# A float32 decoder layer on one core: seven products of halves in place of eight in its projections, with the sums of the weights made on GpSimd

## The reference

```
h = rms_norm(x)
proj = h @ w_in            # (1024, 1024) x (1024, 10256)
(gq, gk, gv, g_low, gr, hq, hf, hi, hg, sz, sxbc, sdt, gates) = split(proj)
y_gla, y_hgrn, y_ssm = three mixers of these (silu of gr, hq, hg, sz; a causal convolution of 4 taps and silu on sxbc)
merged = sum of sigmoid(gates[i]) * (y_i @ w_br[i]);  x = x + merged @ w_out
h2 = rms_norm(x); router: softmax over 4 groups (top 1), 8 experts in it (top 2)
x = x + weights * SwiGLU experts of h2;   out = rms_norm(x)
```

## Time and profile before

| | |
|---|---|
| time, median of 3 runs | 2144.92 us (2144.08 to 2148.81) |
| the profiled execution | 2143.66 us, its span 2142.0 us |
| TensorE busy, weight loads busy | 1979.7 us (92%), 1621.3 us |
| VectorE, ScalarE, GpSimd busy | 1337.7, 921.4, 362.7 us |
| granted TensorE clock, mean | 0.971 |
| HBM | 211 GB/s over the span |

### The profile page before, as it was taken

One profiled execution on the slowest core, in us unless ns is written; L12 is line 12 of the kernel. 1 busy time (PEld: TensorE's weight loads), 2 busy tenths in 40 slices (PEclk: granted clock), 3 DMA queues, 4 the chain that ended last, 5 costly groups with the idle time before them and its releaser, 6 DMA issues. The chain is left out here.

```text
span 2142.0 us, 26814 instructions
## 1 busy us (share of the span) xinstructions
PE 1979.7 (92%) x10826; PEld 1621.3 (76%) x10827; DVE 1337.7 (62%) x1475; ACT 921.4 (43%) x998; POOL 362.7 (17%) x203
## 2 busy tenths in 40 slices
PE   6999999999999999999997999986699999999994
PEld 5778888888987777777775787865588888888872
DVE  5930000576215777877874565556698999999974
ACT  4211010112114444444443334231578888878863
POOL 4223232243310000000001000012122222222210
PEclk9999999999999999999998999998799999999997
DMA  5242222224236553565645754451799999999986
GB/s 160 82 157 98 99 98 79 78 79 137 80 103 151 151 165 120 147 157 161 149 121 187 258 216 162 154 206 60 293 367 382 386 391 384 388 386 388 386 328 247
DMA packets 217236, 435.97 MB, mean 204 GB/s; under 512 B 27730, under 2 KB 150754, under 8 KB 189602
## 3 DMA queue, kind: packets, MB, share of 16 engines
q1 hardware_dynamic: 185954, 361.97, 49.3%
q10 hardware_dynamic: 20288, 51.39, 6.7%
...
HBM read 369.67 MB, written 81.43 MB: 211 GB/s over the span
## 5 line engine op out<-in xcount | busy, mean ns | idle before, releaser
L636 DVE TENSOR_SCALAR tap<-u,taps 128x1024 f32<-128x1024 f32 x16 | 20.1, 1297 | 293.1 <-ACT u L594 293.1
L666 PE MATMUL ps<-h_hi,w_hi 128*128 128x512 f32 x576 | 178.1, 391 | 2.4 <-PEq L58 2.4
L666 PE MATMUL ps<-h_hi,w_lo 128*128 128x512 f32 x576 | 177.8, 390 | 0.0
L666 PE MATMUL ps<-h_lo,w_hi 128*128 128x512 f32 x576 | 177.7, 390 | 0.0
L2416 DVE TENSOR_TENSOR gu_lo<-gate_raw,gu_hi 128x2048 fp32r<-128x2048 f32 x64 | 146.6, 2293 | 32.8 <-ACT gu_hi L2361 32.7
L1311 PE MATMUL psum<-h_hi,l_hi 128*128 128x512 f32 x384 | 158.7, 413 | 3.5 <-PEq L58 3.5
L1311 PE MATMUL psum<-h_lo,l_hi 128*128 128x512 f32 x384 | 160.1, 417 | 0.0
L1311 PE MATMUL psum<-h_hi,l_lo 128*128 128x512 f32 x384 | 157.5, 410 | 0.0
L2416 DVE TENSOR_TENSOR gu_lo<-up_raw,gu_hi 128x2048 fp32r<-128x2048 f32 x64 | 146.4, 2287 | 13.7 <-ACT gu_hi L2361 13.7
L2421 DVE TENSOR_TENSOR dn_lo<-dn_raw,dn_hi 128x2048 fp32r<-128x2048 f32 x62 | 142.0, 2292 | 16.4 <-ACT dn_hi L2371 13.2
L604 ACT ACTIVATE out<-ps 128x2048 f32<-128x2048 f32 x14 | 26.4, 1883 | 270.2 <-PE ps L666 201.2
...
## 6 DMA issues: line engine op xcount, KB each, us to landing
...
```

The costliest lines, as they stand in the source:

```text
L666: ins = nc.tensor.matmul(ps[b][:, a * T + half * 512:a * T + half * 512 + 512], w[:, k, a * P:(a + 1) * P], h[:, k, half * 512:half * 512 ...
```

## The change

The weights and h are cut into halves. For one pair of 128-column tiles, the weights are four blocks of 512 rows by 128 columns, and h is four quarters of 512 channels by 512 tokens. The four output quarters came from eight products of such blocks. Now (`step` on each engine) they come from seven: of blocks and of sums and differences of blocks. The four sums of h (`th`, `tl`) are made once, by VectorE and ScalarE (`rows`, `rows_hi`, `rows_split`), those of the weights in every step by GpSimd (`summed`). Seven products (`g` 0 to 6) go to the three PSUM banks X, Y and Z; the partial sums of X and Y are read out in between, by ScalarE (snapshots) and VectorE (`added`), and the third, fifth and seventh product (`g` 2, 4, 6) wait for that (`snap_ready`, `c_ready`). ScalarE now makes the upper parts of the weights (`upper`), VectorE the rest (`lower`), and both for step n+1 while step n's products run. The silu and the convolution steps take turns (convolution at n = 1, 3, ..., 15), and the taps of step n-1 run in step n (`tap`); their first one moved to ScalarE (`conv_first`). Two of the `tokens` steps come first and two last. The four loops are written out.

Other edits: in `norm1_and_decays` two PSUM tiles take turns, and ScalarE casts two upper parts; each block makes its own `ident`; `y` and `gates` have another order in HBM, so that a load reads longer rows; in `merge_and_route` the turned rows and logits of the first chunks run one step later (`beside`), `rest_w` for the last step comes before `gated`, and records and weights of the choice are made ahead of `places`; `recs` is loaded before the work list is stored; two blocks end without the drain of GpSimd; `finish` adds chunks 2, 3, 5, 6 on TensorE and no more 1, 3, 4, 6.

```diff
+        def turn_ps(c):
+            return acc[2][:] if c < NCH // 2 and c % 2 else tr[:]
...
-            upper_part(2)
-            upper_part(3)
             upper_w(1)
             for c in range(4, NCH):
+                pool.wait_ge(hi_ready, c)
...
+            def upper_part(c):
+                act.wait_ge(hf_ready, c + 1)
+                nc.scalar.copy(h_hi[:, :, c * CH:(c + 1) * CH], h_f[c % 2][:]).then_inc(hi_ready, 1)
...
+    COLS = [TOKENS[0], TOKENS[1]] + STEPS + [TOKENS[2], TOKENS[3]]
...
+        X, Y, Z = ([ps[b][:, i * S:(i + 1) * S] for b in range(2)] for i in range(3))
...
+        def source(n, g):
+            return (block_of(n, 0, 0), sum_w, sum_w, block_of(n, 0, 1), block_of(n, 1, 0), block_of(n, 0, 1), block_of(n, 1, 1))[g]
...
+            def summed(n, i):
...
+                if i == 0:
+                    loaded(pool, n + HEAD)
+                    if n:
+                        pool.wait_ge(split_ready, G * n)
+                    nc.gpsimd.tensor_tensor(sum_w, block_of(n, 1, 0), block_of(n, 1, 1), ALU.add).then_inc(s_ready, 1)
+                elif i == 1:
+                    pool.wait_ge(split_ready, G * n + 2)
+                    nc.gpsimd.tensor_tensor(sum_w, sum_w, block_of(n, 0, 0), ALU.subtract).then_inc(s_ready, 1)
+                elif i == 2:
+                    pool.wait_ge(s_ready, 4 * n + 2)
+                    nc.gpsimd.tensor_tensor(block_of(n, 1, 0), block_of(n, 0, 0), block_of(n, 1, 0), ALU.subtract).then_inc(s_ready, 1)
+                else:
+                    pool.wait_ge(split_ready, G * n + 4)
+                    nc.gpsimd.tensor_tensor(block_of(n, 0, 1), block_of(n, 0, 1), sum_w, ALU.subtract).then_inc(s_ready, 1)
...
+            def upper(n, g):
...
+                if n:
+                    act.wait_ge(group_done, G * (n - 1) + g + 1)
+                else:
+                    act.wait_ge(tok_done, 1 if g < FRONT else 2)
+                if g in (1, 2, 4, 5):
+                    act.wait_ge(s_ready, 4 * n + (1, 2, 4, 5).index(g) + 1)
+                else:
+                    loaded(act, n + HEAD)
+                nc.scalar.copy(slot_hi[g], source(n, g)).then_inc(hi_ready, 1)
...
+            def conv_first(n, a):
...
+                nc.scalar.activation(row(n, a), u[a][:, 0:T], ACT.Copy, scale=tap_col(n, a, 0)).then_inc(tap_ready, 1)
+            def conv_out(n, a):
+                act.wait_ge(conv_ready, 2 * convs(n) + a + 1)
+                nc.scalar.activation(row(n, a), row(n, a), ACT.Silu, bias=tap_col(n, a, SSM_CONV)).then_inc(out_ready, 1)
...
+            def step(n):
+                b, before = n % 2, is_conv(n - 1)
+                act.wait_ge(group_done, G * n + 1)
+                if is_conv(n):
+                    if convs(n):
+                        act.wait_ge(conv_ready, 2 * convs(n))
+                else:
+                    row_free(act, n)
+                nc.scalar.copy(place(n, 0, 0), X[b]).then_inc(snap_ready, 1)
+                upper(n + 1, 0)
+                act.wait_ge(group_done, G * n + 2)
+                nc.scalar.copy(place(n, 1, 1), Y[b]).then_inc(snap_ready, 1)
+                upper(n + 1, 1)
+                act.wait_ge(group_done, G * n + 3)
+                nc.scalar.copy(place(n, 0, 1), X[b]).then_inc(snap_ready, 1)
+                for g in (2, 3, 4):
+                    upper(n + 1, g)
+                if before:
+                    conv_out(n - 1, 0)
+                upper(n + 1, 5)
+                if not is_conv(n):
+                    act.wait_ge(c_ready, 3 * n + 3)
+                    nc.scalar.activation(row(n, 0), row(n, 0), ACT.Silu).then_inc(out_ready, 1)
+                    send(n, 0)
+                act.wait_ge(group_done, G * n + 7)
+                if is_conv(n):
+                    nc.scalar.copy(place(n, 1, 0), X[b]).then_inc(x_read, 1)
+                else:
+                    nc.scalar.activation(place(n, 1, 0), X[b], ACT.Silu).then_inc(x_read, 1)
+                upper(n + 1, 6)
+                if is_conv(n):
+                    conv_first(n, 0)
+                    conv_first(n, 1)
+                else:
+                    nc.scalar.activation(place(n, 1, 1), place(n, 1, 1), ACT.Silu).then_inc(out_ready, 1)
+                    act.wait_ge(x_read, n + 1)
+                    send(n, 1)
+                if before:
+                    conv_out(n - 1, 1)
...
+            for n in range(N):
+                step(n)
+            tokens_hi(N + HEAD, 2)
+            act.wait_ge(c_ready, 3 * N)
+            tokens_hi(N + HEAD + 1, 3)
+            tokens_out(N + HEAD, 2)
...
+            def lower(n, g):
+                if n >= N:
+                    return
+                dve.wait_ge(hi_ready, G * n + g + 1)
+                ins = tt(slot_lo[g], source(n, g), slot_hi[g].bitcast(F32), ALU.subtract).then_inc(split_ready, 1)
+                if g == G - 1:
+                    dve.wait_ge(split_ready, G * n + G)
+                    dve.sem_inc(prepared, 1)
+            def added(n, i):
+                b = n % 2
+                dve.wait_ge(group_done, G * n + (4, 5, 6)[i])
+                dve.wait_ge(snap_ready, 3 * n + (1, 2, 3)[i])
+                bank, a, half = ((Z, 0, 0), (X, 1, 1), (Y, 0, 1))[i]
+                tt(place(n, a, half), bank[b], place(n, a, half), ALU.add).then_inc(c_ready, 1)
+            def tap(n, a, k):
+                if not is_conv(n):
+                    return
+                if k == 1:
+                    dve.wait_ge(tap_ready, 2 * convs(n) + a + 1)
+                    if a == 0:
+                        dve.wait_ge(c_ready, 3 * n + 3)
+                    else:
+                        dve.wait_ge(x_read, n + 1)
+                ins = nc.vector.scalar_tensor_tensor(row(n, a), u[a][:, k:k + T], tap_col(n, a, k), row(n, a),
+                                                     ALU.mult, ALU.add)
+                if k < SSM_CONV - 1:
+                    own.link(ins)
+                else:
                     ins.then_inc(conv_ready, 1)
+            def step(n):
+                m = n + 1
+                tap(n - 1, 0, 1)
+                lower(m, 0)
+                tap(n - 1, 0, 2)
+                lower(m, 1)
+                tap(n - 1, 0, 3)
+                lower(m, 2)
+                tap(n - 1, 1, 1)
+                added(n, 0)
+                lower(m, 3)
+                tap(n - 1, 1, 2)
+                added(n, 1)
+                lower(m, 4)
+                tap(n - 1, 1, 3)
+                added(n, 2)
+                lower(m, 5)
+                lower(m, 6)
...
+                moving = (rows_of(0, 0), (th[0], tl[0]), (th[1], tl[1]), rows_of(1, 0), (th[2], tl[2]), rows_of(1, 1), (th[3], tl[3]))
+                for g, (bank, first) in enumerate(((X, True), (Y, True), (X, False), (Z, True), (X, False), (Y, False), (X, False))):
+                    pe.wait_ge(split_ready, G * n + g + 1)
+                    if g == 0:
+                        if n < 2:
+                            pe.wait_ge(tok_read, n + 1)
+                        else:
+                            pe.wait_ge(x_read, n - 1)
+                            pe.wait_ge(c_ready, 3 * (n - 2) + 3)
+                    if n == 0 and g == 1:
+                        pe.wait_ge(t_split, 4 * KH)
+                    if g == 2:
+                        pe.wait_ge(snap_ready, 3 * n + 1)
+                    if g == 4:
+                        pe.wait_ge(snap_ready, 3 * n + 3)
+                    if g == 6:
+                        pe.wait_ge(c_ready, 3 * n + 2)
+                    hi, lo = moving[g]
+                    for k in range(KH):
+                        for q, (w, h) in enumerate(((slot_hi[g], hi), (slot_hi[g], lo), (slot_lo[g], hi))):
+                            ins = nc.tensor.matmul(bank[b], w[:, k, :], h[:, k, :], start=first and k == 0 and q == 0,
+                                                   stop=k == KH - 1 and q == 2, skip_group_check=True)
+                    ins.then_inc(group_done, 1)
...
+    def beside(n):
+        return 2 <= n - DM < 2 + HC
...
+            sp.wait_ge(scattered, 16 * 2 * NCH)
+            sp.dma_start(recs[:], dr["table"].rearrange("(s e) w -> s e w", e=N_EXPERTS)[0:SLAB]).then_inc(recs_in, 16)
             sp.wait_ge(work_ready, 1)
             sp.dma_start(dr["work"], work_i[0:16, :]).then_inc(work_stored, 16)
             sp.wait_ge(work_stored, 16)
-            sp.wait_ge(scattered, 16 * 2 * NCH)
-            sp.dma_start(recs[:], dr["table"].rearrange("(s e) w -> s e w", e=N_EXPERTS)[0:SLAB]).then_inc(recs_in, 16)
...
-                L(tt(w2[:, 0:n], w1[:, 0:n], e2[:, 0:n], ALU.mult))
+                L(nc.vector.tensor_copy(rec[:, 0, cs, 2].bitcast(F32), w1[:, 0:n]))
+                L(tt(rec[:, 1, cs, 2].bitcast(F32), w1[:, 0:n], e2[:, 0:n], ALU.mult))
...
-                for pick, (o1, ix, r, w) in enumerate(((oh1, i1, r1, w1), (oh2, i2, r2, w2))):
-                    cs = slice(c0, c0 + n)
```

(31 more changed lines are left out.)

457 lines of the change are left out of this document (280 added, 177 removed).

## The result

The changed kernel takes 2130.09 us (median of 4 runs, 2128.5 to 2130.31) against 2145.88 of the kernel before (4 runs, 2144.08 to 2148.81): a ratio of 0.9924, 95% interval 0.9906 to 0.9941. Measured a second time, among the experiments, it was 0.9921 (0.9905 to 0.9937). So it is 16 us faster, where the forecast was 41, and 2130 lies outside the range of 2085 to 2124. The profiled execution takes 2130.31 us with a span of 2128.3, clock 0.961.

The account below looks back on a forecast made before the run. The prediction took TensorE, busy for 1979.7 of 2142 us, as the bound. Its terms summed to -41.3 us from the profiled 2143.66, giving 2102.4 (stated as 2103), with a range of 2085 to 2124.

Parts of the forecast that it names:

- Fewer products: In `project`, 84 matmuls of 512 columns a step instead of 96, over 18 steps at 0.2267 us each: -49.0 us.
- Waits in convolution steps: In `project`, TensorE waits 0.1 us at the seventh product and about 1.1 in the next step: +10 us (0 to 24).
- VectorE's load of 18.6: In `project`, VectorE's work in a tap step, with GpSimd's sums holding it off for 4.6 us: 18.6 of 19.04 us.
- rival 3: In `project`, GpSimd's sums make VectorE late, TensorE waits 4 us per tap step, 32 instead of 10: 2124 us; chance 0.20.
- Tail: End of `project`: TensorE stands 6.3 us for the third `tokens` step's cast and split, plus 1.7 of half clock: +8 us.
- norm: In the norm, two PSUM tiles and a product needing four turned chunks bring the first product forward: -2 us (0 to -4).
- Mixers: In the mixers, GpSimd builds `ident` before VectorE can go on: +0.5 us (0 to 1).
- Ends of blocks: Behind routing and experts, from SyncE's last issue to the next block, less drain time: -2 us (0 to -3).
- Routing to experts: Between routing and experts, second scatter, `recs` and gather start earlier: -3.4 us (-2 to -5).
- Merge and w_out: In merge and w_out, two old waits, 6.5 us together, become one of about 8: 0 us (+2 to -4).
- Finish: In `finish`, chunk 1 on VectorE removes most of its 3.94 us wait for matmuls: -3.4 us (-2 to -3.9).
- rival 4: In `project`, waits in every step reach 2.4 us and slow the clock, 74 us instead of 10: 2166 us; chance 0.06.

Follow-up runs that it names:

- small_sums: The changed kernel with GpSimd's four sums a step over a quarter of their elements, so its output is not the layer's: 2121.41 us, ratio 0.9871.
- double_sums: The changed kernel with an idle addition, which nobody reads, ahead of each of GpSimd's four sums a step: 2147.23 us, ratio 0.9993.
- the two repairs: The changed kernel with the last step's rows kept in the convolution's tiles (2122.99 us), and, separately, with the third `tokens` step's weights cast earlier (2120.96 us).
- ident_first: The changed kernel with GpSimd making the identity first in the mixers, not behind the seven masks: 2120.21 us, ratio 0.9865.
- drains: The changed kernel with GpSimd's drain put back at the ends of two blocks: 2121.12 us, ratio 0.9874.
- w_out: The changed kernel with VectorE making the first batch's gate weights behind the splits of the third and fourth weights of w_out: 2130.44 us, ratio 0.9924.

## Why the prediction failed

The direction and the mechanism of the main gain were right; the size was not. The step that failed is the sum's small terms. Four of them came out worse than forecast: the mixers (+12.5 us for +0.5), the ends of blocks (+4.6 for -2), merge and `w_out` (+5.2 for 0) and the tail of `project` (+15 for +8). In the first and the last I had not followed who else waits for an object that moved or is shared. The waits in the convolution steps came out smaller (4 for 10).

- **Fewer products, -49.0**: right in kind. 1512 matmuls, no clock falls in the steps. They start 0.228 us apart and not 0.2267, some 2 us in all, lost in the seventh and the first product of each step; why, stays open.
- **Waits in convolution steps, +10**: they are there at the two places named, behind every tap step but the last, which runs into the wait of 6.50 us. With the slower starts behind them they cost 0.14 and 0.4 us instead of 0.1 and 1.1, 4 us in all by small_sums (8 x 0.5). ScalarE took its snapshot 5.0 us into the next step, where I had laid out 5.9: VectorE's third addition ended at 19.1 of the step and not at 19.5, and the step itself was 0.3 longer. The step of the working that failed is VectorE's load of 18.6: GpSimd's sums hold it off for 1.3 us and not for 4.6. Some 2 us of them fall where VectorE waits for ScalarE's casts, part of them beside the additions that read PSUM, and where a tap runs already it is GpSimd that waits. The lock itself, and rival 3's remark that it costs where taps and sums meet, double_sums confirms.
- **Tail, +8**: the wait I named is there with 5.88 us (6.3 in the forecast, where its three parts make 6.2). Missed is another 6.50 at the third product of step 17, behind a store. I had followed buffers of weights and PSUM, not the output tile of the one step that breaks the alternation. With both, and two spells at half clock, the tail costs 15 by the two repairs. The spells cost about 2.1 us behind the first wait (its product takes 4.79 us for 2.72) and 1.4 behind the second (7.3 less 5.88); the forecast has 1.7 for one.
- **Head of `project`, 0**; **norm, -2** (-2.2): right.
- **Mixers, +0.5**: the failed term that weighs most, +12.5 measured, 12.0 of which are gone in ident_first. I asked only when VectorE needs it. TensorE needs it 7 us into the block, and it is made last.
- **Ends of blocks, -2**: wrong in sign, +4.6 by SyncE's rows. I took a gain from a bound of 0 to -3 and did not consider a loss. The trace of before has GpSimd's drains, 2.03 us from 1498.4 and 5.28 us from 2099.7, the first of them over before SyncE's last issue; so one had nothing to give, and the other only what it outlasts SyncE.
- **Routing to experts, -3.4**: from the end of the last product with `w_out` to the gathered rows 36.97 us before, 31.41 in drains, 34.19 after. It gives 5.6 with the drain back, half of which the drain's place takes away again. The term was right in kind and too small.
- **Merge and w_out, 0**: +5.2 (from the first product of the stage to the end of the last, 311.56 before, 316.79 after). One wait of 8 for two, as laid out, is 7.70. TensorE's long waits here, added up, are 16.8 before and 20.0 after: ScalarE's `h2T` is waited for 6.18 us and not 4.34, and ahead of the turn of the last chunk but one there are now 2.05 us where there were 0.72. The other 2.3 are TensorE's own work, 294.38 us busy for 292.05 with the same number of matmuls, at a mean clock of 0.96 for 0.97. In w_out the same stretch takes 312.78 us, so part of the 5.2 is what differs between executions; no experiment takes these apart.
- **Finish, -3.4**: -2.6; VectorE's wait of 3.94 is down to 0.30 and 1.02:

```profile
2104.96 1.22 DVE L3001 TENSOR_TENSOR x_kept<-x_kept,both 128x1024 f32<-128x1024 f32 x1 [0.30 <-PE both L2984]
...
2108.39 1.22 DVE L3001 TENSOR_TENSOR x_kept<-x_kept,both 128x1024 f32<-128x1024 f32 x1 [1.02 <-PE both L2984]
```

Of the 28 us that the profiled execution lacks of the forecast, 12 stand in the mixers, 10 in merge, routing and the two ends, 4 in `project`, 2 elsewhere. None of the rivals is what happened. Rival 3's time, 2124, is near, and not for its reason: convolution steps lose 4 us, not 32. Nor does rival 4 appear where its waits are made: in double_sums TensorE waits 1.70 us in eight steps and the clock stays at 1.00. The Trainium skill (TensorE: Matmul & The Clock Gate, HAM oscillation) warns of such a loop; waits of this size did not start it here.
